# Start order, feed-forward order, an earlier transpose for the second expert block, and unread products on TensorE

## What is computed

```python
# first_block: token mixing, then experts
h = rms_norm(x, norm_mix_g)
... = split_cols(h @ w_in)            # forgetting attention and sparse attention, 8 heads each
mix = sigmoid(g_a) * out_a + sigmoid(g_b) * out_b
x = x + mix @ w_out
x = x + hierarchical_moe(rms_norm(x, norm_ffn_g), ...)   # 16 experts, two a token, width 512
# second_block
f = swiglu(rms_norm_2(h, ffn1_pre_g), ffn1_w_gu, ffn1_w_down)   # width 2816
h = h + 0.5 * rms_norm_2(f, ffn1_post_g)
z = rms_norm_2(h, mix_pre_g) @ w_in   # neighbourhood attention and latent attention
h = h + rms_norm_2(concatenate([...]) @ w_out, mix_post_g)
f = swiglu(rms_norm_2(h, ffn2_pre_g), ffn2_w_gu, ffn2_w_down)
h = h + 0.5 * rms_norm_2(f, ffn2_post_g)
```

## Time and profile before

| | |
|---|---|
| median of three executions | 1979.58 us (1977.93 to 1980.55) |
| the profiled execution | 1979.71 us |
| its span, first to last instruction | 1977.9 us |
| TensorE busy with products | 1811.5 us, 92% |
| VectorE, ScalarE busy | 966.3 us (49%), 858.6 us (43%) |
| mean granted clock of TensorE | 0.947 |
| chain that ended last, on TensorE | 83% |

### The profile page before, as it was taken

How to read it: one execution, slowest core, us unless ns; L and a number is a source line. 1 busy time by engine, 2 the same in 40 slices (tenths; PEclk the granted TensorE clock), 3 DMA queues, 4 the chain that set the end, 5 groups by cost and what they waited for, 6 DMA issues and landing times.

```text
span 1977.9 us, 22533 instructions
## 1 busy us (share of the span) xinstructions
PE 1811.5 (92%) x8483; PEld 1428.6 (72%) x8483; DVE 966.3 (49%) x1548; ACT 858.6 (43%) x1355; POOL 254.5 (13%) x313
## 2 busy tenths in 40 slices
PE   6997999999859999969999999898788989999997
PEld 5785566666748888857888888786564768888886
DVE  2536444435358999964332342634555353413434
ACT  4234555553237888853222222424566142213222
POOL 3100342320001111110000000331223000000000
PEclk8998899999969999988999999998789989999999
DMA  5323111113568999672323322233000123233331
GB/s 161 107 67 107 43 44 43 44 43 117 202 232 328 383 386 391 264 248 76 107 85 96 106 85 96 87 108 112 12 22 22 46 77 102 85 96 107 87 104 53
DMA packets 161283, 246.31 MB, mean 125 GB/s; under 512 B 11586, under 2 KB 117281, under 8 KB 148256
## 3 DMA queue, kind: packets, MB, share of 16 engines
q1 hardware_dynamic: 152880, 232.30, 34.8%
q0 software_dynamic: 8304, 12.69, 2.1%
HBM read 239.15 MB, written 12.61 MB: 127 GB/s over the span
## 4 chain that ended last, share of the span: by engine, by line
PE 83%; DVE 6%; ACT 4%; issue 3%; DMA 1%; POOL 1%; SPq 0%; DVEq 0%; ACTq 0%; POOLq 0%
PE psum L425 24%; PE psum L426 23%; PE psum L427 23%; PE psum L570 3%; PE psum L590 3%; PE psum L559 2%; ACT warea_r L410 2%; DVE warea_r L416 1%; PE psum L1232 1%; DMA warea<-in_w_in 1%; POOL arena L690 1%; PE psum L1138 1%; PE psum L1020 1%; DVE xarea L2214 1%; PE psum L1401 0%
## 5 line engine op out<-in xcount | busy, mean ns | idle before, releaser
L416 DVE TENSOR_TENSOR warea_r<-warea,warea_r 128x2048 fp32r<-128x2048 f32 x114 | 268.0, 2353 | 388.7 <-ACT warea_r L410 388.5
L425 PE MATMUL psum<-tarea_r,warea_r 128*128 128x512 f32 x896 | 358.2, 400 | 5.9 <-DVE arena_r L2235 3.9
L426 PE MATMUL psum<-tarea_r,warea_r 128*128 128x512 f32 x896 | 351.7, 393 | 0.0
L427 PE MATMUL psum<-tarea_r,warea_r 128*128 128x512 f32 x896 | 351.4, 392 | 0.0
L410 ACT ACTIVATE warea_r<-warea 128x2048 fp32r<-128x2048 f32 x114 | 217.2, 1907 | 303.2 <-PE psum L427 288.4
L425 PE MATMUL psum<-warea_r,arena_r 128*128 128x512 f32 (+1 forms) x768 | 300.8, 392 | 15.1 <-DVE arena_r L2180 7.3
L427 PE MATMUL psum<-warea_r,arena_r 128*128 128x512 f32 (+1 forms) x768 | 297.2, 387 | 0.0
L426 PE MATMUL psum<-warea_r,arena_r 128*128 128x512 f32 (+1 forms) x768 | 297.1, 387 | 0.0
L425 PEld LDWEIGHTS psum<-tarea_r,warea_r 128*128 128x128 f32 x896 | 169.5, 189 | 48.3 <-issue 7.7
L427 PEld LDWEIGHTS psum<-tarea_r,warea_r 128*128 128x128 f32 x896 | 169.9, 190 | 36.3
L426 PEld LDWEIGHTS psum<-tarea_r,warea_r 128*128 128x128 f32 x896 | 169.8, 190 | 34.1 <-issue 0.7
(11 more groups left out here) (321 smaller groups left out, 2436.2 us busy)
## 6 DMA issues: line engine op xcount, KB each, us to landing
warea<-in_ffn_w_gu SPq DMA_DIRECT2D x88, 512.0 KB, 4.9
warea<-in_w_in SPq DMA_DIRECT2D x48, 512.0 KB, 4.7
warea<-in_ffn_w_down SPq DMA_DIRECT2D x40, 512.0 KB, 4.4
arena<-in_w_up SPq DMA_DIRECT2D x16, 1024.0 KB, 7.3
tarea<-in_w_up SPq DMA_DIRECT2D x16, 1024.0 KB, 7.7
tarea<-in_w_down SPq DMA_DIRECT2D x16, 1024.0 KB, 8.0
warea<-in_w_gate SPq DMA_DIRECT2D x14, 1024.0 KB, 7.8
harea<-in_w_gate SPq DMA_DIRECT2D x14, 1024.0 KB, 8.1
```

The source lines that it names most:

```text
L416: dve.tensor_tensor(w_lo[:, u % 2, :], raw[:, u % RAW, :], w_hi[:, u % 2, :].bitcast(f32), ALU.subtract)\
L425: nc.tensor.matmul(out, high, by_high, start=first, stop=False)
L426: nc.tensor.matmul(out, high, by_low, start=False, stop=False)
L427: return nc.tensor.matmul(out, low, by_high, start=False, stop=last)
```

## The change

- **Beginning.** Units 0 to 3 get places of their own in the arena (`EARLY`), so units 0 to 5 are loaded without waiting for a split. Unit 0 is issued behind x's second tile; SyncE waits for x's fourth tile before unit 1 and the constants; POOL waits for x's fourth tile and unit 0 before all its loads but the first gain column.
- **Feed-forwards.** `row_factor` goes behind chunk 0; both splits of unit `v + 2` go behind the chunk's own steps.
- **Second expert block.** `slot_features(1)` goes into `gate_up(0)`, behind its third weight part, and ScalarE's `slot_high(1)` waits for all of `gate_up(0)`.
- **Unread products.** `keep_busy(bank, n, cols)` issues `n` float32 products into a bank whose content nobody reads: 6 ahead of `slot_features(0)`, and 12, 5 and 3 ahead of the transposes for the first feed-forward, the attention and the second feed-forward; for the first feed-forward also 3 of 128 columns ahead of each tile but the first.
- Two semaphores are merged, and the two adds a tile in L2214 are chained by the engine's own step semaphore. POOL's loads of the bias table use one semaphore in place of three.

```diff
--- before.py
+++ after.py
@@ -162,6 +162,7 @@
 AT_MID = AT_FFN1 + 2 * UNITS
 AT_FFN2 = AT_MID + 14
 RAW = 2
+EARLY = 4
 JOBS = ([("ga", j) for j in range(8)] + [("fu", j) for j in range(8)] + [("gb", j) for j in range(8)]
         + [("nu", j) for j in range(8)])
...
@@ -401,19 +402,28 @@
         sem, value = through[u]
         eng.wait_ge(s[sem], i + value)
+    def raw_of(u):
+
+        return carve(2048 * u, 2048) if u < EARLY else raw[:, u % RAW, :]
+
+    def unit_in(u):
+
+        return (s[f"early{u}"], 32) if u < EARLY else (raw_in[u % RAW], 32 * ((u - EARLY) // RAW + 1))
+
     def split_high(u, i=0):
         act = nc.scalar
-        act.wait_ge(raw_in[u % RAW], 32 * (u // RAW + 1) + (i * 16))
+        sem, value = unit_in(u)
+        act.wait_ge(sem, value + (i * 16))
         if u >= 2:
             unit_through(act, u - 2, i)
-        act.activation(w_hi[:, u % 2, :], raw[:, u % RAW, :], ACT.Copy).then_inc(s["split_hi"], 1)
+        act.activation(w_hi[:, u % 2, :], raw_of(u), ACT.Copy).then_inc(s["split_hi"], 1)
     def split_low(u, i=0):
         dve = nc.vector
         dve.wait_ge(s["split_hi"], i + (u + 1))
-        dve.tensor_tensor(w_lo[:, u % 2, :], raw[:, u % RAW, :], w_hi[:, u % 2, :].bitcast(f32), ALU.subtract)\
+        dve.tensor_tensor(w_lo[:, u % 2, :], raw_of(u), w_hi[:, u % 2, :].bitcast(f32), ALU.subtract)\
             .then_inc(s["split_lo"], 1)
     def weights(u, at, n):
@@ -729,26 +739,28 @@
         def _(sp):
             def piece(u, at, src):
                 k, cols = src.shape[1], src.shape[2]
-                return raw[:, u % RAW, at:at + k * cols].rearrange("p (c n) -> p c n", c=k)
+                return raw_of(u)[:, at:at + k * cols].rearrange("p (c n) -> p c n", c=k)
             def feed(u):
-                if u >= RAW:
+                if u >= EARLY + RAW:
                     sp.wait_ge(s["split_lo"], u - RAW + 1)
                 for at, width, src in units[u]:
                     k, cols = src.shape[1], src.shape[2]
                     if width == 288 and cols == 8:
-                        dst = raw[:, u % RAW, 0:k * width].rearrange("p (c n) -> p c n", c=k)[:, :, at:at + cols]
+                        dst = raw_of(u)[:, 0:k * width].rearrange("p (c n) -> p c n", c=k)[:, :, at:at + cols]
                     else:
-                        dst = raw[:, u % RAW, at:at + k * width].rearrange("p (c n) -> p c n", c=k)[:, :, 0:cols]
-                    sp.dma_start(dst, src).then_inc(raw_in[u % RAW], 16)
+                        dst = raw_of(u)[:, at:at + k * width].rearrange("p (c n) -> p c n", c=k)[:, :, 0:cols]
+                    sp.dma_start(dst, src).then_inc(unit_in(u)[0], 16)
             masks = NCONST - CONSTS["na_mask"][1]
             sp.dma_start(const[:, 0:P], w["consts"][:, 0:P]).then_inc(s["ident_in"], 16)
             for t in range(NT):
                 sp.dma_start(xres[:, t, :], w["x"][0, t * P:(t + 1) * P, :]).then_inc(s[f"rows_in{t}"], 16)
-            for u in range(2):
-                feed(u)
+                if t == 1:
+                    feed(0)
+            sp.wait_ge(s["rows_in3"], 16)
+            feed(1)
             sp.dma_start(const[:, P:masks], w["consts"][:, P:masks]).then_inc(s["const_in"], 16)
             for u in range(2, AT_MIX):
                 feed(u)
@@ -760,7 +772,7 @@
             for u in range(AT_OUT + 2, AT_FFN1):
                 feed(u)
             sp.wait_ge(s["gate_scaled"], 16)
-            sp.dma_start(const[:, masks:NCONST], w["consts"][:, masks:NCONST]).then_inc(s["mask_in"], 16)
+            sp.dma_start(const[:, masks:NCONST], w["consts"][:, masks:NCONST]).then_inc(s["const_in"], 16)
             def expert_unit(b, i, e):
@@ -892,6 +904,8 @@
                 nc.gpsimd.tensor_tensor(hn[:, 0, :], hn[:, 0, :], gain, ALU.mult).then_inc(s["premul_pool"], 1)
             gain_column(0, "norm_mix_g", "col_in0")
+            pool.wait_ge(s["rows_in3"], 16)
+            pool.wait_ge(s["early0"], 32)
             for k, name in enumerate(("fox_q_g", "fox_k_g", "nsa_q_g", "nsa_k_g")):
                 for a in (0, 64):
                     pool.dma_start(gcol[a:a + 64, k:k + 1], w[name].rearrange("a d -> d a")).then_inc(s["head_gain_in"], 16)
@@ -1011,10 +1024,18 @@
         @block.tensor
         def _(pe):
-            def raw_features(k, ready):
+            def keep_busy(bank, n, cols=512):
+
+
+                for _ in range(n):
+                    nc.tensor.matmul(bank[:, 512 - cols:512], ident, upper[:, 0:cols], start=True, stop=True)
+
+            def raw_features(k, ready, between=0):
                 for t in range(NT):
+                    if t:
+                        keep_busy(ps[KD - 1], between, P)
                     ready(t)
                     for c in range(KD):
                         mm = nc.tensor.transpose(ps[c][:, P * t:P * t + P], xres[:, t, P * c:P * c + P], ident)
@@ -1246,6 +1267,8 @@
                             mm.then_inc(s["moe_done"], 1)
                     if i == 0 and isinstance(b, int) and b == 1:
                         hidden_features(0)
+                    if i == 2 and isinstance(b, int) and b == 0:
+                        slot_features(1)
             def hidden_features(b):
                 pe.wait_ge(s["hb_ready"], b + 1)
@@ -1272,11 +1295,12 @@
                 first = isinstance(b, int) and b == 0
                 gate_up(b)
-                slot_features(b + 1)
                 if not first:
+                    slot_features(b + 1)
                     down(b - 1, 4)
                     hidden_features(b)
+            keep_busy(ps[6], 6)
             slot_features(0)
             for b in range(STATIC):
                 expert_round(b)
@@ -1301,14 +1325,14 @@
                     elif g % 2:
                         pe.wait_ge(s["f_evac"], evac - 8 + 2 * v + 2)
                     for k in range(2):
-                        if g % 2 == 0 and isinstance(v, int) and v == 1 and k:
-                            row_factor((2, 4)[g // 2], ps[7])
                         for c in range(KD):
                             if g % 2 == 0 and isinstance(v, int) and v == 0 and k == 0:
                                 pe.wait_ge(s["hT_low_ready"], low0 + c + 1)
                             mm = products(ps[2 * (v % 2) + k], *weights(u, 1024 * k + P * c, P),
                                           hT_hi[:, c, :], hT_lo[:, c, :], c == 0, c == KD - 1)
                     mm.then_inc(s["unit_done"], 1)
+                    if g % 2 == 0 and isinstance(v, int) and v == 0:
+                        row_factor((2, 4)[g // 2], ps[7])
                 low0 = (8, 0, 24, 0)[g]
                 for v in range(3):
@@ -1342,7 +1366,8 @@
                     if j + n < HALF:
                         mm.then_inc(s["unit_done"], 1)
-            raw_features(2, lambda t: pe.wait_ge(s["res_ready"], 4 + t + 1))
+            keep_busy(ps[7], 12)
+            raw_features(2, lambda t: pe.wait_ge(s["res_ready"], 4 + t + 1), 3)
             ffn_half(0)
             ffn_half(1)
             pe.wait_ge(s["f_evac"], 16)
@@ -1355,6 +1380,7 @@
                     pe.wait_ge(s["na_tab"], g)
                 nc.tensor.matmul(bank[:, 0:384], flip, xrev[:, g, :], start=True, stop=True).then_inc(s["tab_psum"], 1)
+            keep_busy(ps[7], 5)
             raw_features(3, lambda t: pe.wait_ge(s["res_ready"], 8 + t + 1))
             for n in range(4):
                 cols = 512 if n < 3 else 416
@@ -1459,6 +1485,7 @@
                                           *weights(u, 512 * c, 512), c == 0, c == 3)
                         mm.then_inc(s["o2_psum"], 1)
             pe.wait_ge(s["f_evac"], 24)
+            keep_busy(ps[7], 3)
             raw_features(4, lambda t: pe.wait_ge(s["res_ready"], 12 + t + 1))
             ffn_half(2)
             ffn_half(3)
@@ -1645,6 +1672,8 @@
             def slot_high(b):
+                if isinstance(b, int) and b == 1:
+                    act.wait_ge(s["moe_done"], 8)
                 for h_ in range(2):
                     act.wait_ge(s["xtr_psum"], 2 * b + (h_ + 1))
                     nc.scalar.activation(XT_hi[:, 4 * h_:4 * h_ + 4, :], ps[2 + h_].rearrange("p (c q) -> p c q", c=4),
@@ -1699,10 +1728,10 @@
                     act.wait_ge(s["ff_scaled"], i + (base + v + 1))
                     nc.scalar.activation(sgb[:, v % 2, :], sgb[:, v % 2, :], ACT.Silu).then_inc(s["ff_silu"], 1)
-                    split_high(u0 + v + 2, i)
                     act.wait_ge(s["gated"], i + (base + v + 1))
                     at = hid_hi[:, v, :] if isinstance(i, int) else hid_hi[:, ds(i + v, 1), :].rearrange("p a q -> p (a q)")
                     nc.scalar.activation(at, sgb[:, v % 2, :], ACT.Copy).then_inc(s["hid_high"], 1)
+                    split_high(u0 + v + 2, i)
                 for v in range(3):
                     if v == 0 and g % 2 == 0:
@@ -2209,11 +2238,12 @@
             for t in range(NT):
                 dve.wait_ge(s[f"rows_in{t}"], 48)
```

(26 more changed lines are left out.)

6 lines of the change are left out of this document (3 added, 3 removed).

## The result

The changed kernel takes 1960.39 us (median of four runs, 1951.37 to 1961.02), the kernel before 1978.76 beside it (four runs, 1975.79 to 1980.55). The ratio is 0.9898, with a 95% interval of 0.9867 to 0.9929: faster by 1.0%, where the forecast was 1956.7 in 1951.5 to 1963.5. The profiled execution took 1960.16, its span is 1958.3, so 19.6 us less than before's, where the sum said 22.95.

A forecast was written before the change was run, and what follows sets the result against it. TensorE was taken as the bound, busy for all but a twelfth of the span, so other engines count only where it waits. The terms sum to 22.95 us off 1979.7, giving 1956.7 us, range 1951.5 to 1963.5.

The forecast's parts named there:

- rival A: Clock not held through transposes: the 1.3, 1.4, 1.0 and 1.8 us are missing, 1962.2 us; chance 0.15.
- three terms of the unread products: Gains at the first expert block (1.4 us), ahead of the first feed-forward (1.0) and at the second feed-forward's transposes (1.8).
- The beginning: New load order lands x's last tile at 12.1 and starts the first product at 14.3 instead of 21.82: 7.5 us.
- rival B: Bandwidth holds the beginning, x's last tile lands at 16.8: 2.8 instead of 7.5, no 1.3, 1962.7 us; chance 0.12.
- The clock's 1.3: At the first products, the middle of 0 and 2.6 us for a cold start at half clock that may go away.
- First expert block: 6 unread products fill the 6.10 us wait for gathered rows, transposes and first products run at full clock: net 1.4 us.
- Second expert block: Transposes moved into the block before; the chain behind ScalarE's copy gets no shorter and begins later: -0.45 us.
- Ahead of the first feed-forward: 12 unread products inside the 15.0 us wait, small ones between tiles; the products behind at full clock: 1.0 us.
- Inside the feed-forwards: Row factor and splits moved: chunk 2's pause and half clock go, 7.4 us; four waits at half ends go, 3.0.
- Transposes: Unread products ahead of attention and the second feed-forward are covered by waits: 0 us and 1.8 us gained.
- Rival C: Unread products run one after the other at half clock, 2.07 us each: slower, 1989 us; chance 0.03.
- rival D: Pauses taken away come back behind later splits and loads, under 4 us stay: 1978 us; chance 0.02.

The follow-up runs named there:

- E9: The changed kernel, but POOL issues its small loads at once again, SyncE's order kept; 1962.27 us, one execution.
- E5: The changed kernel with the second expert block's transposes back behind the first block and ScalarE's copy no longer waiting for the block's end; 1957.23 us, one execution.
- E2: The changed kernel with the beginning alone put back as before the change; 1963.87 us, ratio 0.9941.
- E4: The changed kernel with all unread products taken out; 1955.16 us, ratio 0.9894.
- E7: The changed kernel without unread products, run a second time; 1959.25 us, ratio 0.9912.
- E11: The changed kernel without unread products, run a third time; 1957.08 us, ratio 0.9909.
- E3: The changed kernel with the old order inside the feed-forwards; 1968.26 us, ratio 0.995. Its rival: the clock does not depend on the 1.97 us pauses.
- E6: The changed kernel with only the two weight splits put back into the middle of a chunk, row factor still moved; 1963.37 us, one execution.
- E10: The changed kernel itself, run a third time beside the one without unread products; 1958.24 us, ratio 0.9902.
- E12: The kernel with eight more places of unread products, without those ahead of both feed-forwards and attention; 1953.37 us, ratio 0.9874.
- E8: The changed kernel with the second block's transposes put back and unread products in eight more places of the first transformer block; 1947.45 us, ratio 0.9848.
- E1: The changed kernel itself, run again; 1959.86 us, ratio 0.9916.

## Why the prediction was right, and what it left out

The time lies in the range, but that is weak evidence for the sum. The measured 1960.39 is nearer to rival A's 1962.2 than to the forecast 1956.7. Without the three terms of the unread products (1.4, 1.0, 1.8) the sum gives 1960.9, in the range too. What the sum says of order, the runs bear out stage by stage. The 4.2 us of the unread products they do not: 0.5 +- 1.2 us of loss over the whole. That the time was still in the range is owed to the range's width.

**The beginning, 7.5 forecast, 7.1 at the first product.** The tile came at 12.2 by the flow without POOL's packets, as chosen; E9 shows that those packets were indeed in the 275 GB/s of the earlier trace rows, and rival B is out. They weigh more than that row lets see: with them the 3.15 MB are there at 15.34, 236 GB/s from 2 us on, where the prediction has 13.5 for them. The clock's 1.3 was too much: half clock lasts 3.7 instead of 5.4 us, which is worth 0.8. With that 7.9 of 8.8 are there, and 8.4 to 9.2 at 113.8.

**First expert block, 1.4 forecast, 1.5 to 2.0 measured** (kernels without the products: about 0). The 6 products took 7.48 us, forecast 7.6:

```profile
557.00 7.48 PE L1031 MATMUL psum<-const 128*128 128x512 f32 x12
564.32 1.05 PE L1253 MATMUL psum<-const,arena 128*128 128x128 f32 x8
566.93 0.50 PE L435 MATMUL psum<-warea_r,arena_r 128*128 128x512 f32 x1 [1.56 <-DVE arena_r L2209]
```

**Second expert block, -0.45 forecast, -0.45 to -0.5 measured**, and 0 in E5. The chain behind ScalarE's copy was the pause, as said.

**Ahead of the first feed-forward, 1.0 forecast, not there in the mean.** The lead grows by 6.9, 7.1 and 2.9 over this stage in three executions of the changed kernel, by 6.8, 7.1 and 3.9 in E2, E5 and E9, which have the same unread products and the same order here: 5.8 in the mean. Without unread products (E4, E7, E11) it is 6.0 to 7.3, 6.5 in the mean. The window at 889.2 shows the full clock that was forecast, but four of the nine traces with these products have half clock there (E3, E6, E9, E10), and two of the five without them (E7, E12) have full clock too. E9's and E7's windows from the first product on:

```profile
892.90:898.70 5.80, 5.76 (x18) 4.62 (x19) 5.45 (x10) 4.40 (x9) 0.00 (x0) 0.71 0.14 39
```

```profile
886.30:892.10 5.80, 5.75 (x25) 4.80 (x26) 5.46 (x10) 4.42 (x9) 0.00 (x0) 1.00 0.14 34
```

So these 12 and 9 products don't decide the clock here, and what does stays open. Only in one of the four, E10, was a load late. There x's fourth tile waits for it:

```profile
885.48 2.61 DVE L2241 SCALAR_TENSOR_TENSOR xarea<-tarea,arena,xarea 128x1024 f32<-128x1024 f32 x2 [1.40 <-DMA tarea<-y_assigned]
...
888.14 1.35 PE L1041 MATMUL psum<-const,xarea 128*128 128x128 f32 x8 [2.24 <-DVE xarea L2241]
890.19 0.77 PE L435 MATMUL psum<-tarea_r,warea_r 128*128 128x512 f32 x1 [0.70 <-DVE tarea_r L1899]
```

The load is 1.4 us late, TensorE pauses 2.24, the first product runs at 0.77 instead of 0.47, so at half clock, and this feed-forward brings that execution 2.9 us. In E3, E6 and E9 no tile waits for a load, and the clock is half all the same. All four had lost 2.8 to 2.9 us of their lead at the end of the expert blocks (below), the other five with these products 0 to 1.65. Whether one brings the other was not tested.

**Inside the feed-forwards, 7.4 + 3.0 forecast.** The leads of the kernels without unread products grow by 5.9 to 6.0 in the second feed-forward; two half ends have 2.1 of that, so 3.9 remain for chunk 2's pause and its clock, forecast 3.7; a wait of 1.97 alone would be half of it, so the clock's part is there, against E3's rival. The mis-sized term is the half ends: 4.2 instead of 3.0. I took the wait of 0.74 for the pause. Products start 0.23 us apart and are shown as 0.39 or 0.40 long (the timeline of E8 above, at 15.11 and 15.34), so 0.16 us of the pause lie under the last product's modelled end. The rest is behind the pause, in the trace before:

```profile
1026.45 0.39 PE L427 MATMUL psum<-warea_r,arena_r 128*128 128x512 f32 x1
1027.59 0.50 PE L425 MATMUL psum<-warea_r,arena_r 128*128 128x512 f32 x1 [0.74 <-DVE arena_r L2235]
1027.92 0.40 PE L426 MATMUL psum<-warea_r,arena_r 128*128 128x512 f32 x1
```

The start at 1027.59 comes 1.14 behind the one before instead of 0.23, and the next one 0.33 behind it instead of 0.23, so 1.0 us is lost; the few starts behind that, up to 0.24 apart, have what is left. For both terms together E3's 9.0 +- 1.4 and the leads (two feed-forwards, 5.95 each) hold the forecast 10.4 between them.

**Transposes, 1.8 forecast for the second feed-forward, 1.7 measured.** The lead grows by 7.7 with the unread products and by 5.9 to 6.0 without, in every trace of either. Last tile ready at 1578.52 + 4.87 = 1583.4, ScalarE's first copy at 1583.87:

```profile
1575.92 2.84 PE L1031 MATMUL psum<-const 128*128 128x512 f32 x6 [0.84 <-DVE harea L2410]
...
1578.52 4.87 DVE L1889 SCALAR_TENSOR_TENSOR xarea<-harea,rstd,xarea 128x1024 f32<-128x1024 f32 x4
...
1583.87 4.73 ACT L1545 ACTIVATE tarea_r<-psum,small 128x512 fp32r<-128x512 f32 x8 [0.49 <-PE psum L1041]
```

The 0.5 between them were 2.2 in the earlier trace rows. Rival A's mechanism is out: the first expert block and the second feed-forward start at full clock behind transposes, the first feed-forward in five of nine traces, and only the very first products do not. But its price came near, since the unread products bring nothing over the whole. Rival C is out too: the 6 products took 1.25 us each (7.48 above), and the 12 ahead of the first feed-forward 10.57 us, 0.88 each, where it needed 1.8. So is rival D: the pauses taken away did not come back. The merged semaphores and the chained adds, forecast 0, were not run by themselves.

**What the sum left out** is what the clock does where nothing was edited. I had counted those stages as unchanged. The attention stage shows it best; its windows, of before, the changed kernel, E4 and E12:

```profile
1331.67:1576.19 244.52, 210.84 (x1030) 146.59 (x1029) 118.39 (x364) 120.20 (x269) 46.81 (x34) 0.87 0.14 43
```

```profile
1318.19:1564.30 246.11, 211.41 (x1030) 147.41 (x1029) 118.68 (x364) 119.75 (x269) 46.70 (x34) 0.88 0.14 42
```

```profile
1317.71:1558.24 240.53, 205.22 (x1030) 143.54 (x1029) 118.20 (x364) 119.93 (x268) 47.06 (x34) 0.91 0.15 43
```

```profile
1304.89:1554.49 249.60, 214.50 (x1030) 149.28 (x1029) 118.76 (x364) 119.77 (x269) 46.73 (x34) 0.86 0.14 42
```

The same 1030 product records, VectorE's and ScalarE's work equal within 0.6 us, and 240.5 to 249.6 us long: the shortest has the highest granted clock, the longest the lowest. Over all 14 traces the mean is 244.1 us with unread products ahead of it (nine) and 244.0 without (five, E12 among them), a difference of 0.1 +- 1.8: no effect of the edit shows, and executions of the same kernel differ by 3.7 (246.1, 246.1 and 242.4 for the changed one). In the profiled execution the untouched stages took back 1.9 + 1.0 + 1.6 = 4.5 us, and 24.1 from the edits less these is the 19.6; E1's execution of the same kernel ends at 23.1.

**Why the unread products do not show in the time.** Two of their places bring what was forecast in every trace, 1.5 to 2.0 and 1.7; ahead of the first feed-forward they bring nothing in the mean. One loss goes with them. At the end of the blocks a pause of 2.65 us stands in all traces; these are E10's and E11's products behind it and the windows of both:

```profile
855.44 0.79 PE L435 MATMUL psum<-warea_r,arena_r 128*128 128x512 f32 x1 [2.65 <-DVE arena_r L2227]
...
855.40:865.00 9.60, 8.59 (x24) 6.48 (x24) 0.00 (x0) 0.85 (x1) 0.83 (x1) 0.68 0.08 29
```

```profile
858.05 0.49 PE L435 MATMUL psum<-warea_r,arena_r 128*128 128x512 f32 x1 [2.65 <-DVE arena_r L2227]
...
858.00:867.60 9.60, 5.71 (x24) 4.43 (x24) 0.86 (x1) 3.71 (x3) 2.63 (x4) 0.94 0.12 47
```

With the 6 products ahead of the first block the clock falls behind it in eight of ten traces, and 1.6 to 2.9 us of the lead that stood at 603.3 go; in the four traces without them it never does. Why stays open: the pause is as long in both, and it comes nearly 300 us after the products. No run moved that pause alone. The rest lies at the beginning of the first feed-forward and in attention, which scatter by more than the gain itself; that the sum comes to 0.5 +- 1.2 us is measured, how it divides is only argued from single traces.

## What to carry to other kernels

Order buys most surely: who stands ahead of whom on a load queue (7 us here) and in an engine's program behind a wait (some 6 us a feed-forward) is there in every execution. Filling pauses with unread products paid in some places (E8's three above, the second feed-forward's transposes) and not in another that had all that is asked for, a pause of 15 us, products that end inside it and work bound by the clock behind it (the first feed-forward). What tells them apart no run shows. It has to be judged by stages of the trace, since one stage's clock scatters by more than one place brings, and by the whole only when several places add up (10.1 +- 1.5 us for eight in E8, by the means, 0.5 of it from the transposes put back). When such a sum is made, keep a term for what the clock does in stages nobody touches, with both signs.

## What the runs showed of the hardware

- Two dozen small loads on POOL's queue delayed 3.1 MB of large ones on SyncE's by 3.1 us (x's last tile at 15.34 in E9, 12.23 without them).
- A stage with equal work took 240.5 us at a mean granted clock of 0.91 and 249.6 at 0.86, and in executions of one and the same kernel 242.4 to 246.1.
- A shown wait of 0.74 us of TensorE cost 1.04 to 1.08.
- The same pause of 2.65 us of the same kernel had half clock behind it in some executions and full clock in others.
- TensorE reached full clock on transposes alone (1273.5 to 1276.0).
